# Reordering the head of a mixer stage and moving a gate table from GpSimd to VectorE

## The chip, the cores and the metric

The kernel runs on one core of a Trainium2 chip. A core has TensorE (PE: matmuls, and transposes through an identity matrix), VectorE (DVE), ScalarE (ACT), GpSimd (POOL) and SyncE (SP), each with its own instruction stream that is worked off in order. The engines meet through semaphores only. The metric is the device time of one execution in microseconds, lower is better.

## The reference

One layer of a decoder for 512 tokens of 1024 features, in f32:

```python
h = x + concat(GatedDeltaNet(u), RG_LRU(u)) @ W_out        # u = rmsnorm(x)
h = h + CrossAttn(rmsnorm(h), rmsnorm(mem))                # 4 heads, 256 memory tokens
h = h + MoE(rmsnorm(h))                                    # top 4 of 32 SwiGLU experts
out = rmsnorm(h)
```

The parts that the change touches are these:

```python
# gated delta rule, per head (4 heads of 128) and chunk
gcum = cumsum(g);  decay = exp(gcum_t - gcum_s) below the diagonal
A = strict_lower((k*beta) @ k.T * decay);  solve (I + A) [u, w] = [v*beta, k*beta*exp(gcum)]
qk = causal(q @ k.T * decay);  o = (q*exp(g)) @ S + qk @ v_new;  S = S*exp(g_last) + k_dec.T @ v_new
# RG-LRU, 4 blocks of 128 channels
r = sigmoid(x @ w_a + b_a);  i = sigmoid(x @ w_x + b_x)
a = exp(8 * r * log_sigmoid(lam));  h_t = a*h_{t-1} + sqrt(1 - a*a) * (i*x)
# routing and experts
logits = rmsnorm(h) @ w_router + b_router;  top_e, gate = top_k(4), softmax
out_e = ((clip(x@w_up+b_up)+1) * gt*sigmoid(1.702*gt)) @ w_down + b_down   # gt = min(x@w_gate+b_gate, 7)
y = sum over the 4 experts of gate * out_e
```

## The kernel before, in words

**Stages.** Front projections; then the mixer (gated delta rule and RG-LRU); the output projection; cross-attention; routing; a loop over blocks of 128 rows, each of one expert; and a last block that shares its end with the combination of the results and the final norm. Weights are f32 and are split on chip into a high and a low part in a reduced format (ACT rounds the high part, DVE subtracts for the low part), and each weight piece is multiplied as high x high, high x low and low x high.

**Order.** Nothing schedules the instructions. Each engine's program is written out by hand, with a `wait_ge(semaphore, count)` ahead of what needs another engine's result and a `then_inc` behind what releases one. So where an instruction stands in its engine's text decides what it delays.

**The head of the mixer.** All heads work on 128-token chunks, four to a head (`[P, 4, P]` tiles of 128x512). PE first does the eight matmuls of the RG gates (L1175) into banks 6 and 7 of the accumulator memory, then for each head the matmul that sums log decays along a chunk (L1181, "decay sums"), for which DVE prepares the operand (L1709). DVE turns the sums into arguments (L1715 to L1719), ACT applies `exp` to them (L828, L829, L833). Then come four products per head on PE (`kk`, `kq`, and two transposes: L1199, L1201, L1203, L1205), and DVE multiplies each with its decay or scale (L1729 to L1739). POOL cuts the triangles with `affine_select` (L502, L504), and builds the masked matrix of a level (L523). The two `fill_wait` calls (L1120) issue dummy matmuls that nothing reads.

**The inverse.** `(I + A)` is inverted in seven levels. Level one is `I - mask*A` for each head (DVE L1744, transposed on PE L1215, copied by ACT L845). The six others are a loop of 24 steps, one per level and head, with two matmul groups and a transpose on PE (L1227, L1239, L1247), two copies on ACT (L852, L855) and a subtraction on DVE. In the first twelve steps DVE also does the RG-LRU (three steps per block). ACT's `tanh` and `exp` of the RG gates (L818, L821) stand ahead of the decay exponentials; its `sqrt` (L859) stands in the loop. A change of function set shows as ACT_TABLE_LOAD.

**Routing.** In the last projection of the cross-attention (PE L1304, weights split by ACT L713 and DVE L1616), four tiles of the result are added to the residual (DVE L1812), transposed (PE L1404), copied to SBUF by `evac_h2` (DVE L1883) and multiplied with the router weights (PE L1411). These steps are put between the pieces by the piece number `c`.

**The expert loop.** SP loads three 4 MB weight matrices per block into a ring (L426). POOL issues the indirect transfers and, block by block, the load of the biases (L629) for PE's bias matmul (L1496). Ahead of the loop's first bias load POOL works out `g_parts` (L608 to L614): per token a row of 32 with the four gate values at their experts. Only the last block needs it, for `y`'s bias term. In the last block DVE splits weight pieces (L1888), adds a bias (L2045), clamps and multiplies (L2056, L2058) and makes the low part of the hidden values (L2061). PE transposes with L1533 and multiplies with L1546.

## Time and profile before

| | us |
|---|---|
| median of 3 runs | 1771.23 (1770.09 to 1771.25) |
| the profiled execution | 1772.93, of which the span is 1771.2 |
| PE busy / DVE busy / ACT busy / POOL busy | 1690.2 / 1437.0 / 1274.6 / 527.8 |
| chain that ended last: PE / DVE / issue / ACT / POOL | 61% / 18% / 12% / 6% / 3% |

The profile is of one execution. A row of a timeline has the start, the busy time of a run of equal instructions, and in brackets the idle time of that engine ahead of it with the instruction that ended it. `PEclk` is the clock that TensorE was granted, as a share of full speed; half speed shows as 0.50. The share of each engine over the whole span says little, since most of the span is the expert loop and the change is in four short places.

### The profile page before, as it was taken

To read this page: it belongs to the slowest core of one execution; us is meant where nothing else is said; L and a number is where in the kernel's file an instruction comes from. 1 tells how busy PE (TensorE), PEld (TensorE's weight loads), DVE (VectorE), ACT (ScalarE), POOL (GpSimd) and SP (SyncE) were. 2 spreads that over 40 slices of the span, in tenths; PEclk is the share of its full clock that TensorE was granted. 3 is DMA by queue.
4 is the path that set the end of the run, shared out by engine and by line. 5 is a ranking of instruction groups with operands and counts; after the bars stand their busy time and mean duration, and the time that the engine had idled before them with its cause. 6 is when DMAs were issued, how large, how long until landed. Compare 5 with 4: busy or idle time off the path is not lost.

```text
span 1771.2 us, 24520 instructions
## 1 busy us (share of the span) xinstructions
PE 1690.2 (95%) x8065; PEld 1385.7 (78%) x8065; DVE 1437.0 (81%) x1531; ACT 1274.6 (72%) x1452; POOL 527.8 (30%) x624
## 2 busy tenths in 40 slices
PE   6999799899899989999999999999999999999997
PEld 3778598787768768888888888888888888888885
DVE  3558686663347969999999999999999999999997
ACT  4453454464435668888888888888888888888885
POOL 3453552200022822242222222232232323232232
PEclk9999999999998989999999999999999999999999
DMA  7312100042014879999999999999999999999993
GB/s 249 119 51 100 41 1 1 24 190 95 26 82 191 330 271 369 360 383 378 355 371 371 382 359 370 360 382 379 351 371 369 379 364 369 360 380 379 353 371 120
DMA packets 53880, 476.18 MB, mean 269 GB/s; under 512 B 10503, under 2 KB 11640, under 8 KB 29266
## 3 DMA queue, kind: packets, MB, share of 16 engines
q1 hardware_dynamic: 42528, 450.70, 62.8%
q0 software_dynamic: 11120, 24.91, 6.3%
q8 instruction: 25, 0.41, 0.1%
q14 instruction: 13, 0.11, 0.0%
q10 hardware_dynamic: 194, 0.06, 0.0%
HBM read 461.24 MB, written 23.08 MB: 273 GB/s over the span
## 4 chain that ended last, share of the span: by engine, by line
PE 61%; DVE 18%; issue 12%; ACT 6%; POOL 3%; DMA 1%; ACTq 0%; POOLq 0%; DVEq 0%
PE ps L1546 20%; PE ps L1506 17%; PE ps L1143 10%; PE ps L1304 4%; DVE wsp L1888 4%; DVE extra L2058 2%; DVE extra L2056 2%; DVE wsp_b L1888 2%; ACT extra L1048 2%; POOL extra L608 1%; PE ps L1533 1%; PE ps L1227 1%; DVE wf L1616 1%; PE ps L1239 1%; PE ps L1496 1%
## 5 line engine op out<-in xcount | busy, mean ns | idle before, releaser
L1888 DVE TENSOR_TENSOR wsp<-ring,wsp 128x1024 fp32r<-128x1024 f32 x512 | 601.1, 1219 | 26.6 <-ACT wsp L1003 26.1
L1003 ACT ACTIVATE wsp<-ring 128x1024 fp32r<-128x1024 f32 x388 | 387.0, 1051 | 80.2 <-PE ps L1488 53.0
L580 POOL TENSOR_TENSOR guard<-guard 1x1 f32<-1x1 f32 x219 | 133.8, 616 | 763.0 <-ACT extra L1071 327.9
L1506 PE MATMUL ps<-wsp,x_hi 128*128 128x512 f32 x1152 | 311.8, 392 | 0.6 <-DVE x_lo L2014 0.6
L1888 DVE TENSOR_TENSOR wsp_b<-ring,wsp_b 128x1024 fp32r<-128x1024 f32 x256 | 301.8, 1218 | 9.8 <-ACT wsp_b L1081 9.1
L1506 PEld LDWEIGHTS ps<-wsp,x_hi 128*128 128x128 f32 x1152 | 217.5, 189 | 50.1 <-issue 1.1
L1003 ACT ACTIVATE wsp_b<-ring 128x1024 fp32r<-128x1024 f32 x194 | 205.5, 1060 | 32.3 <-PE ps L1506 11.0
L1506 PE MATMUL ps<-wsp,x_lo 128*128 128x512 f32 x576 | 179.1, 392 | 0.0
L1616 DVE TENSOR_TENSOR wf<-ring,wf 128x1024 fp32r<-128x1024 f32 x64 | 81.3, 1273 | 111.8 <-ACT wf L713 111.8
L713 ACT ACTIVATE wf<-ring 128x1024 fp32r<-128x1024 f32 x80 | 84.2, 1055 | 117.4 <-PE ps L1143 62.2
L1143 PE MATMUL ps<-act_hi,wf 128*128 128x512 f32 x512 | 161.6, 397 | 2.6 <-DVE wf L1616 2.1
L1081 ACT ACTIVATE wsp<-ring 128x1024 fp32r<-128x1024 f32 x124 | 131.9, 1064 | 36.8 <-PE ps L1546 36.8
L1546 PE MATMUL ps<-wsp_b,hid_hi 128*128 128x512 f32 x512 | 140.2, 395 | 0.0
L1506 PE MATMUL ps<-wsp_b,x_hi 128*128 128x512 f32 x512 | 136.8, 389 | 0.0
L1546 PE MATMUL ps<-wsp,hid_hi 128*128 128x512 f32 x512 | 136.8, 389 | 0.0
L1506 PEld LDWEIGHTS ps<-wsp,x_lo 128*128 128x128 f32 x576 | 108.6, 189 | 23.4
L1488 PE MATMUL ps<-wsp,x_hi 128*128 128x512 f32 x384 | 118.2, 389 | 0.0
L1143 PEld LDWEIGHTS ps<-act_hi,wf 128*128 128x128 f32 x512 | 95.7, 188 | 27.5 <-issue 8.1
L1546 PEld LDWEIGHTS ps<-wsp,hid_hi 128*128 128x128 f32 x512 | 96.1, 188 | 20.0
L1506 PEld LDWEIGHTS ps<-wsp_b,x_hi 128*128 128x128 f32 x512 | 96.1, 188 | 20.0
L1546 PEld LDWEIGHTS ps<-wsp_b,hid_hi 128*128 128x128 f32 x512 | 93.6, 188 | 22.8 <-issue 4.8
L1143 PE MATMUL ps<-act_lo,wf 128*128 128x512 f32 x256 | 99.8, 390 | 0.0
(380 smaller groups left out, 2993.9 us busy)
## 6 DMA issues: line engine op xcount, KB each, us to landing
ring<-in_w_gate_dram SPq DMA_DIRECT2D x32, 4096.0 KB, 15.3
ring<-in_w_up_dram SPq DMA_DIRECT2D x32, 4096.0 KB, 14.4
ring<-in_w_down_dram SPq DMA_DIRECT2D x32, 4096.0 KB
ring<-in_w_in_dram SPq DMA_DIRECT2D x6, 2048.0 KB, 12.0
ring<-in_w_ckv_dram SPq DMA_DIRECT2D x4, 2048.0 KB, 10.1
ring<-in_w_out_dram SPq DMA_DIRECT2D x2, 2048.0 KB, 10.6
ring<-in_w_cq_dram SPq DMA_DIRECT2D x2, 2048.0 KB, 11.1
ring<-in_w_co_dram SPq DMA_DIRECT2D x2, 2048.0 KB, 10.6
```

The lines of the kernel that those rows point to most:

```text
L580: return pool.tensor_tensor(guard[:, i:i + 1], guard[:, 0:1], guard[:, 0:1], ALU.mult)
L713: act.activation(parts_of(f, 0), piece(f), ACT.Copy).then_inc(wfh_ready, 1)
L1003: act.activation(split_w(c, 0), ring[:, m, k], ACT.Copy).then_inc(hi_ready, 1)
L1048: act.activation(gs, ps[:, 0:2, :].rearrange("p b f -> p (b f)"), ACT.Sigmoid, scale=1.702).then_inc(sg_ready, 1)
L1081: act.activation(split_w(c, 0), ring[:, GM, c], ACT.Copy).then_inc(hi_ready, 1)
L1143: last = pe.matmul(o, parts_of(f, w)[:, k], a[:, k], start=(k == 0 and w == 0 and a is a_hi), stop=(k == KT - 1 and a is a_lo))
L1304: last = pe.matmul(ps[:, banks[b]], a[:, rows + kk, ts], parts_of(f, w)[:, kk], start=(first and kk == 0 and a is a_hi and w == 0), stop=( ...
L1488: o = pe.matmul(ps[:, bank + i], xp[:, c % KT * P:(c % KT + 1) * P], split_w(c, w)[:, i * 512:(i + 1) * 512], start=False, stop=(last_k an ...
L1506: last = pe.matmul(ps[:, 2 * j + i], xp[:, k * P:(k + 1) * P], split_w(c, part)[:, i * 512:(i + 1) * 512], start=False, stop=(k == KT - 1 ...
L1546: last = pe.matmul(ps[:, 4 + i], xp[:, k * P:(k + 1) * P], split_w(c, part)[:, i * 512:(i + 1) * 512], start=(k == 0 and xp is hid_hi and ...
L1616: dve.tensor_tensor(parts_of(f, 1), piece(f), parts_of(f, 0), ALU.subtract).then_inc(wfl_ready, 1)
L1888: dve.tensor_tensor(split_w(c, 1), ring[:, (GM + c // KT) % 3, c % KT], split_w(c, 0), ALU.subtract).then_inc(lo_ready, 1)
```

## The change

1. PE: the decay sums stand ahead of the RG gate matmuls. Those go into banks 0 and 1, two or four at a time, between the products of the heads. The transposes of the first level follow head by head in the same stretch (into banks 2, 3, 6 and 7). Both `fill_wait` calls (30 and 34 dummy matmuls) are gone. The level loop's first steps wait for one head each and not for all four.
2. ACT: the decay exponentials stand ahead of the gates' sigmoids. `tanh` and `exp` of the gates move into the level loop (`tanh` in steps 0 to 3, `exp` in steps 3 and 5).
3. POOL: the `affine_select` of `a_m` is dropped, that of `qkt` moves into the masks of level 2. The mask of the first level is done head by head. Two of four gated inputs move behind masks of the loop.
4. DVE: `first_level(h-1)` follows the products of head h; DVE waits for the decays and not for the triangles.
5. DVE: the second `evac_h2` stands at c == 10 and not at c == 11.
6. The gate table is removed from POOL and built by DVE with 15 instructions ahead of the last block's `expert_lo`.

In the diff a part of the indentation is left off.

```diff
@@
...
         y_m, qkt = extra[:, 0:4], extra[:, 4:8]
+        D_A, D_K, D_Q = (1, 4, 7, 9), (2, 5, 8, 10), (3, 6, 11, 12)
+        X1_BANK = (2, 3, 6, 7)
         def onrm(h):
@@
         pool.tensor_tensor(b_lo, b_f, b_hi, ALU.subtract).then_inc(bias_split, 1)
-for n in range(4):
+def gated_input(n):
     pool.wait_ge(ri_ready, 2 * n + 2)
     pool.tensor_tensor(chan[:, 16 + n], chan[:, 16 + n], act_t[:, 4 + n], ALU.mult).then_inc(bx_ready, 1)
+def level_mask(l, h):
+    pool.tensor_tensor(quart(as_m[:, (4 * l + h) % 2]), quart(a_m[:, h]),
+                       lmask[:, l:l + 1, :].to_broadcast([P, 4, P]), ALU.mult).then_inc(as_ready, 1)
 for h in range(H):
-    pool.wait_ge(decay_ready, 3 * h + 2)
...
+    pool.wait_ge(decay_ready, D_Q[h])
     pool.wait_ge(kk_done, 4 * h + 2)
...
-pool.wait_ge(kk_evac, 4 * H)
-for l in range(7):
+    pool.wait_ge(kk_evac, 4 * h + 1)
+    pool.wait_ge(gb_done, H)
+    if h >= 2:
+        pool.wait_ge(x1_ready, h - 1)
+    level_mask(0, h)
+gated_input(0)
+gated_input(1)
+for l in range(1, 7):
     for h in range(H):
         i = 4 * l + h
...
-                           lmask[:, l:l + 1, :].to_broadcast([P, 4, P]), ALU.mult).then_inc(as_ready, 1)
+        if i - 4 >= 2:
+            pool.wait_ge(qm_done, i - 5)
+        else:
+            pool.wait_ge(x1_ready, H)
+        level_mask(l, h)
+        if i in (5, 6):
+            gated_input(i - 3)
+        if l == 2:
+            pool.wait_ge(kk_evac, 4 * h + 2)
+            pool.affine_select(out=quart(qkt[:, h]), in_=quart(qkt[:, h]), compare_op=ALU.is_ge, fill=0.0,
+                               base=0, pattern=[[0, 4], [1, P]], channel_multiplier=-1).then_inc(masked_ready, 1)
 for h in range(H):
@@
 link(take(0, tok_tab, slice(CAP, CAP + 1)))
...
-pool.wait_ge(codes_ready, 2)
...
-for t in range(0, NT, 2):
-    for u in range(2):
-        for k in range(TOPK):
-            last = pool.tensor_scalar(one[:, u, k], e_row, top_e[:, t + u, k:k + 1], gates[:, t + u, k:k + 1], ALU.is_equal, ALU.mult)
-    link(last)
...
@@
         sums_of(j - 6)
-act.wait_ge(proj_done, 24)
+act.wait_ge(gp_ready, 1)
+act.activation(egp, gp, ACT.Exp).then_inc(kdf_ready, 1)
+def q_decay(h):
+    act.wait_ge(kd_in, h + 1)
+    if h >= 2:
+        act.wait_ge(qexp_ready, h - 1)
+    act.activation(q_m[:, h % 2], ps[:, h], ACT.Exp).then_inc(decay_ready, 1)
+for h in range(H):
+    act.wait_ge(split_ready, h + 1)
+    act.activation(a_m[:, h], a_m[:, h], ACT.Exp, scale=-1.0).then_inc(decay_ready, 1)
+    act.activation(qkt[:, h], qkt[:, h], ACT.Exp).then_inc(decay_ready, 1)
+    if h < 2:
+        q_decay(h)
+act.wait_ge(kd_in, H)
+act.activation(kdf, kdf, ACT.Exp).then_inc(kdf_ready, 1)
+q_decay(2)
+q_decay(3)
 for n in range(4):
     for g in range(2):
         act.wait_ge(gate_mm, 2 * n + g + 1)
         r = (R_BA if g == 0 else R_BX) + n
-        act.activation(act_t[:, 4 * g + n], ps[:, 6 + g], ACT.Sigmoid, bias=par[:, r:r + 1]).then_inc(ri_ready, 1)
...
-for n in range(4):
+        act.activation(act_t[:, 4 * g + n], ps[:, g], ACT.Sigmoid, bias=par[:, r:r + 1]).then_inc(ri_ready, 1)
+def rg_tanh(n):
     act.wait_ge(bx_ready, n + 1)
     act.activation(act_t[:, 4 + n], act_t[:, n], ACT.Tanh, scale=nrate[:, n:n + 1]).then_inc(rt_ready, 1)
-act.wait_ge(rt_ready, 4)
-for n in range(4):
+def rg_exp(n):
+    act.wait_ge(rt_ready, n + 1)
     act.activation(act_t[:, n], act_t[:, n], ACT.Exp, scale=rate[:, n:n + 1]).then_inc(rt_ready, 1)
...
 def rg_hi(n):
     act.wait_ge(rg_done, n + 1)
@@
     if 2 <= i < 22:
         act.wait_ge(x1t_done, H + i - 1)
         act.activation(x_m[:, (i - 2) % 4], ps[:, 3 * (i % 2) + 2], ACT.Copy).then_inc(x_lev, 1)
+    if i < 4:
+        rg_tanh(i)
+    if i in (3, 5):
+        rg_exp(i - 3)
+        rg_exp(i - 2)
     if i in (4, 7, 10, 13):
         n = i // 3 - 1
         act.wait_ge(mult_in, n + 1)
@@
         pe.matmul(ps[:, 6 + i % 2], ones[:], chan[:, 16 + i], start=True, stop=True).then_inc(l2_done, 1)
-pe.wait_ge(rgw_in, 32)
-pe.wait_ge(tile_done, 20)
-for n in range(4):
-    for g in range(2):
-        if n > 0:
-            pe.wait_ge(ri_ready, 2 * (n - 1) + g + 1)
-        pe.matmul(ps[:, 6 + g], rgw[:, g, n], chan[:, 16 + n], start=True, stop=True).then_inc(gate_mm, 1)
 pe.wait_ge(tile_done, 24)
 for h in range(H):
     pe.wait_ge(gu_ready, h + 1)
     pe.matmul(ps[:, h], ones[:], as_m[:, h % 2], start=True, stop=True).then_inc(gb_done, 1)
-pe.wait_ge(qk_ready, 2 * H)
-for h in range(H):
-    if h == 1:
-        pe.wait_ge(decay_ready, 3)
-        pe.wait_ge(kd_in, 1)
-        fill_wait(30, 0)
+def rg_gates(n):
+    for g in range(2):
+        if n > 0:
+            pe.wait_ge(ri_ready, 2 * (n - 1) + g + 1)
+        pe.matmul(ps[:, g], rgw[:, g, n], chan[:, 16 + n], start=True, stop=True).then_inc(gate_mm, 1)
+def head_products(h):
...
         last.then_inc(kk_done, 1)
-pe.wait_ge(decay_ready, 3 * H)
-pe.wait_ge(kd_in, H)
-fill_wait(34, 0)
-for h in range(H):
+def first_inverse(h):
     pe.wait_ge(x1_ready, h + 1)
...
     last.then_inc(x1t_done, 1)
+pe.wait_ge(qk_ready, 2 * H)
+head_products(0)
+pe.wait_ge(rgw_in, 32)
+pe.wait_ge(decay_ready, D_Q[1])
+rg_gates(0)
+head_products(1)
+head_products(2)
+pe.wait_ge(decay_ready, D_Q[3])
+pe.wait_ge(kd_in, H)
+first_inverse(0)
+rg_gates(1)
+head_products(3)
+first_inverse(1)
+rg_gates(2)
+rg_gates(3)
+pe.wait_ge(kk_evac, 4 * H)
+first_inverse(2)
+first_inverse(3)
+pe.wait_ge(ri_ready, 8)
 def level_q(i):
...
     if i < 4:
-        pe.wait_ge(y1_ready, 4)
+        pe.wait_ge(y1_ready, i + 1)
     else:
         pe.wait_ge(y_lev, i - 3)
...
@@
...
 dve.wait_ge(beta_ready, 1)
-dve.wait_ge(kdf_ready, 2)
+dve.wait_ge(kdf_ready, 1)
 link(dve.tensor_tensor(beg, beta, egp, ALU.mult))
+def first_level(h):
+    dve.wait_ge(as_ready, h + 1)
+    dve.tensor_tensor(quart(x_m[:, h]), ident[:].unsqueeze(1).to_broadcast([P, 4, P]), quart(as_m[:, h % 2]), ALU.subtract).then_inc(x1_ready, 1)
 for h in range(H):
...
     dve.wait_ge(kk_done, 4 * h + 1)
-    dve.wait_ge(masked_ready, 2 * h + 1)
+    dve.wait_ge(decay_ready, D_A[h])
...
     dve.wait_ge(kk_done, 4 * h + 2)
-    dve.wait_ge(masked_ready, 2 * h + 2)
+    dve.wait_ge(decay_ready, D_K[h])
...
     dve.wait_ge(kk_done, 4 * h + 3)
...
+    if h == 0:
+        dve.wait_ge(kdf_ready, 2)
...
     dve.wait_ge(kk_done, 4 * h + 4)
     dve.tensor_tensor(quart(chan[:, 8 + h]), quarters(7), bc(beta), ALU.mult).then_inc(kk_evac, 1)
-for h in range(H):
-    dve.wait_ge(as_ready, h + 1)
...
+    if h >= 1:
+        first_level(h - 1)
+first_level(3)
 for i in range(24):
     h = i % 4
     dve.wait_ge(p_done, i + 1)
-    dve.wait_ge(y1_ready, 4)
+    dve.wait_ge(y1_ready, min(i + 1, 4))
...
         if i % 3 < 2:
@@
     if c == 9:
         evac_h2(0, 0, 4, 1)
         evac_h2(0, 1, 5, 2)
-    if c == 11:
+    if c == 10:
         evac_h2(1, 0, 6, 3)
         evac_h2(1, 1, 7, 4)
     if c == 13:
@@
...
+def gate_table():
+    one = extra[:, 5, 256:512].rearrange("p (t k e) -> p t k e", t=2, k=TOPK)
+    for t in range(0, NT, 2):
+        for u in range(2):
+            ins = dve.tensor_tensor(one[:, u], e_row.unsqueeze(1).to_broadcast([P, TOPK, E]),
+                                    tf4[:, t + u].unsqueeze(2).to_broadcast([P, TOPK, E]), ALU.is_equal)
+        link(ins)
+        for u in range(2):
+            ins = dve.tensor_tensor(one[:, u], one[:, u], gates[:, t + u].unsqueeze(2).to_broadcast([P, TOPK, E]), ALU.mult)
+        link(ins)
+        for u in range(2):
+            ins = dve.tensor_reduce(g_parts[:, t + u, 2 * E:3 * E], one[:, u].rearrange("p k e -> p e k"), AX_X, ALU.add)
+        link(ins)
+    for c in range(2):
+        ins = dve.tensor_copy(g_parts[:, :, E * c:E * (c + 1)].bitcast(F32R), g_parts[:, :, 2 * E:3 * E])
+    link(ins)
+    dve.tensor_tensor(g_parts[:, :, 2 * E:3 * E], g_parts[:, :, 2 * E:3 * E], g_parts[:, :, 0:E], ALU.subtract).then_inc(iota_ready, 1)
 def expert_lo(n, last=False):
...
@@
     for c in range(NSPLIT):
...
+gate_table()
 expert_lo(n_more, last=True)
 dve.wait_ge(bias_split, 4)
...
```

PE's order at the head of the mixer, before: 1175 are the gates, 1181 the decay sums, 1120 the dummies, 1199 to 1205 a head's products.

```order
L1175 MATMUL ps<-chan,xn 128x512 x8
L1181 MATMUL ps<-ring,ones 128x512 x4
L1199 MATMUL ps<-chan 128x128 x4
L1201 MATMUL ps<-chan 128x128 x4
L1203 MATMUL ps<-ident,chan 128x128 x4
L1205 MATMUL ps<-ident,chan 128x128 x4
L1120 MATMUL ps<-sel 128x256 x30
L1199 MATMUL ps<-chan 128x128 x4
```

The same place now: 1179 are the decay sums, 1198 to 1204 a head's products, 1187 the gates, 1211 the first level's transposes.

```order
L1179 MATMUL ps<-ring,ones 128x512 x4
L1198 MATMUL ps<-chan 128x128 x4
L1200 MATMUL ps<-chan 128x128 x4
L1202 MATMUL ps<-ident,chan 128x128 x4
L1204 MATMUL ps<-ident,chan 128x128 x4
L1187 MATMUL ps<-chan,xn 128x512 x2
L1198 MATMUL ps<-chan 128x128 x4
L1200 MATMUL ps<-chan 128x128 x4
```

The eight gate matmuls no longer stand ahead of the decay sums, and the dummies are gone. ACT's order at the start of the level loop, before: 845 copies the first level, 852 and 855 are the loop's copies, 859 the square root.

```order
L845 ACTIVATE extra<-ps 128x512 x4
L852 ACTIVATE ring<-ps 128x512 x3
L855 ACTIVATE ring<-ps 128x512
L852 ACTIVATE ring<-ps 128x512
L855 ACTIVATE ring<-ps 128x512
L852 ACTIVATE ring<-ps 128x512
L855 ACTIVATE ring<-ps 128x512
L859 ACT_TABLE_LOAD
L859 ACTIVATE act_t<-act_t 128x512
```

The same place now: 854 and 857 are the copies, 834 a `tanh`, 838 an `exp`, 866 a square root.

```order
L854 ACTIVATE ring<-ps 128x512
L857 ACTIVATE ring<-ps 128x512
L834 ACTIVATE act_t<-act_t,small 128x512
L838 ACT_TABLE_LOAD
L838 ACTIVATE act_t<-act_t,small 128x512 x2
L854 ACTIVATE ring<-ps 128x512
L857 ACTIVATE ring<-ps 128x512
L866 ACT_TABLE_LOAD
L866 ACTIVATE act_t<-act_t 128x512
L854 ACTIVATE ring<-ps 128x512
L857 ACTIVATE ring<-ps 128x512
L838 ACT_TABLE_LOAD
```

Eight activations and three table loads now stand between the loop's copies. DVE's order around the second `evac_h2`, before: 1616 is the low part of a weight piece, 1812 the addition to the residual, 1883 the copy of `evac_h2`.

```order
L1598 RECIPROCAL small<-small 128x1
L1616 TENSOR_TENSOR wf<-ring,wf 128x1024
L1812 TENSOR_TENSOR resid<-resid,ps 128x512 x2
L1883 COPY chan<-ps 128x4x128 x2
L1616 TENSOR_TENSOR wf<-ring,wf 128x1024 x2
```

The same place now, where 1633 is the low part, 1838 the addition and 1909 the copy.

```order
L1615 RECIPROCAL small<-small 128x1
L1909 COPY chan<-ps 128x4x128 x2
L1633 TENSOR_TENSOR wf<-ring,wf 128x1024
L1838 TENSOR_TENSOR resid<-resid,ps 128x512 x2
L1633 TENSOR_TENSOR wf<-ring,wf 128x1024 x2
```

The two copies stand ahead of one weight piece and one addition that they stood behind.

## Rows read from the trace of the kernel before

**Rows 1.** Windows: start:end, length, busy PE, PEld, DVE, ACT, POOL, PEclk, DMA share, GB/s

```profile
218.00:220.00 2.00, 1.39 (x7) 0.99 (x5) 0.00 (x0) 1.17 (x2) 1.95 (x2) 0.50 0.00 0
...
222.00:276.00 54.00, 53.09 (x457) 51.94 (x456) 46.42 (x53) 30.41 (x52) 29.68 (x22) 0.98 0.00 1
...
627.60:666.80 39.20, 39.01 (x165) 31.94 (x166) 31.66 (x30) 31.38 (x33) 8.51 (x14) 0.92 0.72 259
666.80:703.00 36.20, 36.05 (x166) 29.65 (x165) 33.59 (x33) 31.18 (x33) 8.74 (x14) 1.00 0.94 368
```

**Rows 2.** Timeline of PE, the bias matmul of block 1

```profile
627.64 1.22 PE L1496 MATMUL ps<-bias,sel 128*128 128x512 f32 x2 [10.47 <-DMA bias<-bias_parts]
```

**Rows 3.** Timeline of POOL ahead of the expert loop

```profile
585.42 17.80 POOL L608 TENSOR_SCALAR extra<-extra,gates 128x32 f32<-128x32 f32 x8
...
616.97 1.31 POOL L614 TENSOR_TENSOR extra<-extra 128x128 f32<-128x128 f32 x1
...
623.37 0.59 POOL L629 DMA_DIRECT2D bias<-bias_parts  x1 [0.44 <-issue]
```

**Rows 4.** DMA issues: what, queue, kind, count, KB each, us to landing

```profile
gate_rows<-gates SPq DMA_DIRECT2D x1, 8.0 KB, 9.9
```

**Rows 5.** Timeline of SP, first expert weights and gates

```profile
584.69 0.37 SPq L419 DMA_DIRECT2D gate_rows<-gates  x1
...
614.27 0.37 SPq L426 DMA_DIRECT2D ring<-in_w_down_dram  x1
```

**Rows 6.** Chain of waits around the router: start, length, what

```profile
532.11 0.87 PE ps L1404 x8
...
543.39 5.20 PE ps L1304 x12
548.59 1.71 PE ps L1411 x16
...
551.20 2.77 PE ps L1304 x12
```

**Rows 7.** Timeline of PE at the router

```profile
540.62 2.77 PE L1411 MATMUL ps<-w_rt,chan 128*128 128x32 f32 x16 [2.18 <-DVE chan L1883]
```

**Rows 8.** Timeline of DVE at the router

```profile
533.52 1.21 DVE L1616 TENSOR_TENSOR wf<-ring,wf 128x1024 fp32r<-128x1024 f32 x1
...
536.85 1.23 DVE L1616 TENSOR_TENSOR wf<-ring,wf 128x1024 fp32r<-128x1024 f32 x1 [2.04 <-ACT wf L713]
...
539.19 1.28 DVE L1883 COPY chan<-ps 128x512 f32<-128x512 f32 x2
```

**Rows 9.** Timeline of DVE at the head of the mixer

```profile
186.56 2.26 DVE L1709 TENSOR_TENSOR ring<-tri,small 128x512 f32<-128x512 f32 x2 [5.46 <-PE ps L1181]
...
196.13 0.77 DVE L1723 TENSOR_TENSOR small<-small 128x16 f32<-128x16 f32 x1 [1.03 <-ACT small L836]
...
210.05 0.68 DVE L1739 TENSOR_TENSOR chan<-ps,small 128x512 f32<-128x512 f32 x1
```

**Rows 10.** Timeline of PE, start of the level loop

```profile
220.17 2.04 PE L1227 MATMUL ps<-extra,ring 128*128 128x128 f32 x8 [0.78 <-ACT extra L845]
```

**Rows 11.** Timeline of ACT, functions of the RG gates

```profile
186.35 2.56 ACT L818 ACTIVATE act_t<-act_t,small 128x512 f32<-128x512 f32 x4
188.92 1.28 ACT L821 ACT_TABLE_LOAD   x1
```

**Rows 12.** Timeline of DVE, one-hot rows of the routing, and the last block

```profile
563.00 0.49 DVE L1920 TENSOR_TENSOR extra<-extra 128x128 f32<-128x128 f32 x2
563.52 0.69 DVE L1924 TENSOR_REDUCE extra<-extra 128x32 f32<-128x128 f32 x2
...
1721.23 4.78 DVE L1888 TENSOR_TENSOR wsp<-ring,wsp 128x1024 fp32r<-128x1024 f32 x4
...
1730.20 1.23 DVE L2045 TENSOR_TENSOR extra<-ps,extra 128x1024 f32<-128x1024 f32 x1
```

**Rows 13.** Timeline of PE near the last block's end

```profile
1742.23 0.75 PE L1533 MATMUL ps<-ident,extra 128*128 128x128 f32 x4 [0.80 <-DVE extra L2058]
```

More of the change, by code:

```diff
@@ L354, in build_layer @@
         nf_row, bd_rows, bd_parts = ring[:, GM, 0, :], ring[:, GM, 1, :], split_w(0, 0)
+        e_row = extra[:, 4, 384:384 + E]
         g_parts, g_stack = extra[:, 4, 0:NT * 3 * E].rearrange("p (t c) -> p t c", t=NT), bias4[0:3 * E, T:2 * T]
@@ L546, in _ @@
             link(pool.tensor_copy(ef[:, 288:418], it_i[:, 288:418]))
-            e_row = extra[:, 4, 384:384 + E]
             link(pool.tensor_copy(ef[:, 0:E], it_i[:, 0:E]))
@@ L601, in _ @@
             gather()
-            pool.wait_ge(codes_ready, 2)
-            top_e = extra[:, 5, 128:160].rearrange("p (t k) -> p t k", t=NT)
-            one = extra[:, 5, 256:512].rearrange("p (t k e) -> p t k e", t=2, k=TOPK)
-            for t in range(0, NT, 2):
-                for u in range(2):
-                    for k in range(TOPK):
-                        last = pool.tensor_scalar(one[:, u, k], e_row, top_e[:, t + u, k:k + 1], gates[:, t + u, k:k + 1], ALU.is_equal, ALU.mult)
-                link(last)
-                link(pool.tensor_tensor(one[:, :, 0:2], one[:, :, 0:2], one[:, :, 2:4], ALU.add))
-                link(pool.tensor_tensor(g_parts[:, t:t + 2, 2 * E:3 * E], one[:, :, 0], one[:, :, 1], ALU.add))
-            for c in range(2):
-                link(pool.tensor_copy(g_parts[:, :, E * c:E * (c + 1)].bitcast(F32R), g_parts[:, :, 2 * E:3 * E]))
-            pool.tensor_tensor(g_parts[:, :, 2 * E:3 * E], g_parts[:, :, 2 * E:3 * E], g_parts[:, :, 0:E], ALU.subtract).then_inc(iota_ready, 1)
             link(pool.memset(gate_sb[:], 0.0))
@@ L844, in _ @@
                 act.wait_ge(x1t_done, h + 1)
-                act.activation(y_m[:, h], ps[:, h], ACT.Copy).then_inc(y1_ready, 1)
+                act.activation(y_m[:, h], ps[:, X1_BANK[h]], ACT.Copy).then_inc(y1_ready, 1)
             for i in range(24):
@@ L1206, in _ @@
                     last.then_inc(kk_done, 1)
-            pe.wait_ge(decay_ready, 3 * H)
-            pe.wait_ge(kd_in, H)
-            fill_wait(34, 0)
-            for h in range(H):
+            def first_inverse(h):
                 pe.wait_ge(x1_ready, h + 1)
                 for c in range(4):
-                    last = pe.transpose(quarters(h)[:, c], quart(x_m[:, h])[:, c], ident[:])
+                    last = pe.transpose(quarters(X1_BANK[h])[:, c], quart(x_m[:, h])[:, c], ident[:])
                 last.then_inc(x1t_done, 1)
+            pe.wait_ge(qk_ready, 2 * H)
[17 more added lines that the diff above has]
+            pe.wait_ge(ri_ready, 8)
             def level_q(i):
@@ L1266, in _ @@
             pe.wait_ge(wt_ready, 4)
+            pe.wait_ge(masked_ready, H)
             for c in range(NT):
@@ L1739, in _ @@
                 dve.tensor_tensor(quart(chan[:, 8 + h]), quarters(7), bc(beta), ALU.mult).then_inc(kk_evac, 1)
-            for h in range(H):
-                dve.wait_ge(as_ready, h + 1)
-                dve.tensor_tensor(quart(x_m[:, h]), ident[:].unsqueeze(1).to_broadcast([P, 4, P]), quart(as_m[:, h % 2]), ALU.subtract).then_inc(x1_ready, 1)
+                if h >= 1:
+                    first_level(h - 1)
+            first_level(3)
             for i in range(24):
@@ L1754, in _ @@
                     if i % 3 == 0:
-                        dve.wait_ge(rt_ready, 8)
+                        dve.wait_ge(rt_ready, n + 1)
                         dve.wait_ge(gate_mm, 8)
@@ L1770, in _ @@
                     elif i % 3 == 1:
+                        dve.wait_ge(rt_ready, 5 + n)
                         link(dve.tensor_tensor_scan(act_t[:, 4 + n], act_t[:, n], chan[:, 16 + n], 0.0, ALU.mult, ALU.add))
```

28 lines of the change are left out of this document (removed).

## The prediction

> **What bounds the kernel now.** I read the windows first. In the level loop of the mixer PE works 53.09 of 54.00 us, and in a block of the expert loop 36.05 of 36.20 [rows 1]: both are bound by PE, and the change removes no product from either. So time can only go where PE waits, and the PE timelines and the chain of waits were read for that, at the four places of the edit.
>
> Start of the expert loop: PE idles 10.47 us at 627.64 for the bias of block 1 [rows 2]. POOL issues that DMA at 623.37, because it builds the gate table first, from 585.42 to 618.28 [rows 3]. The window of block 1 is 39.20 long at a granted clock of 0.92, the next 36.20 at 1.00 [rows 1]: after the stall PE ran at half clock (1.2 of 2.4 GHz) for a while.
>
> Router: PE idles 2.18 us at 540.62 for DVE's second `evac_h2` [rows 7], whose copies start at 539.19 behind a weight piece and an addition, although the transposes that they copy ended at 532.98 [rows 6, 8].
>
> Head of the mixer: DVE wrote its first two operands by 181.10 and idled 5.46 us for PE's first decay sum, which stood behind the gates; at 196.13 it waited 1.03 more for ACT [rows 9], which first did four `tanh`, a table load and four `exp` [rows 11]. The level loop began at 220.17 [rows 10].
>
> Last block: DVE is fuller than elsewhere. From 1721.23 to 1730.20, 8.97 us, it does seven pieces of about 1.14 (4.63 to 4.78 for four), 7.95 us [rows 12], so some 1.0 us is free; soon after, PE waits 0.80 for DVE's L2058 [rows 13].
>
> **A. Table off POOL: -13.4.** POOL comes to the loop's first bias load without the 32.86 us from 585.42 to 618.28. It first waits for the gate rows to be written: issued at 584.69, landing 9.9 later [rows 4, 5], at 594.6. Its steps from the table's end to the bias issue took 623.37 - 618.28 = 5.1, so the issue comes at 599.7; the landing took at most 627.64 - 623.37 = 4.3, so 604.0. PE could have used the bias at 627.64 - 10.47 = 617.17. The cover is 13 us. The whole stall goes (10.47), and with it the half-clock stretch: 39.20 - 36.20 = 3.00, of which I count 2.9, since blocks differ by 0.1. What would be late next is a weight matrix. The third of block 1 is issued at 614.27 [rows 5]; 4 MB at the loop's 368 GB/s [rows 1] are 11.4 us, so it is there by about 628 with its latency, and is used in the last third of the block, from 641. Bounds: -10.5 (the clock falls all the same) to -13.5.
>
> **B. Second `evac_h2` one piece earlier: -5.7.** DVE is free at 533.52 + 1.14 = 534.7 and idles until 536.85, and the pair of copies takes 1.28 [rows 8]: done by 536.0, ahead of the 538.44 (540.62 - 2.18) at which PE wants them. The 2.18 go. The stall was followed by half clock: the router matmuls took 2.77 and those of the next group 5.20, against 1.71 and 2.77 later [rows 6]. That gives back 1.06 and 2.43. Sum 5.67. Nothing behind the copies comes later: they fill an idle time, and the piece at 536.85 keeps its place. Bounds: 0 (PE then waits for the next low part instead) to -5.7; the nearest row is the stall itself, so I take the latter.
>
> **C. Mixer: -7.5.** Start: without the gates ahead, the first decay sum runs when DVE has written its operand, about 181.1, so DVE's second pair of L1709 starts some 4.7 to 5.2 earlier (a sum itself lasts under 1 us). The 1.03 for ACT goes, because the decay exponentials come first. Of L1723's 0.77 for sixteen elements a part may go too, which I put at 0 to 0.6. So the products of the heads begin 7.0 earlier (6.3 to 7.3): at 189.9, not 196.9. Before, they ended at 210.73 [rows 9], 13.8 for four heads. Now four first-level subtractions of 0.6 stand between them (2.4), and PE's gate matmuls and POOL's masks fall into the same stretch: 2.0 for stalls, by estimate, between 0 and 1.0 for each head. End 208.1. From the last product to the loop lay 220.17 - 210.73 = 9.4, mostly masks, subtractions and transposes one behind another; of that only the last head's is left, 2.2, and 1.3 for POOL's gated inputs, which stand ahead of the first mask of the loop. The loop starts at about 211.5: -8.7, bounds -5 and -10.
>
> Loop: four `tanh`, four `exp` of 0.64 and three table loads of 1.28 [rows 11] are 9.0 us more for ACT in the first eight of 24 steps. ACT is busy 30.41 of 54.00 [rows 1], so in eight steps (18 us) about 8 are free, more in the first two, which have fewer copies. Only what comes at once delays PE: two `exp` behind a load, 2.6, against the 2.25 of a step (54.00 / 24). Twice 0.4 and a little for the third load is +1.2, with -2 and +3 as bounds: below nothing, since PE ran at half clock from before 218 until about 224 [rows 1], 2 us that need not recur.
>
> The Trainium skill speaks against this part: "ScalarE: Activation LUTs", section "Table sets: the hidden batching unit", asks for all `exp` together and then all square roots, and the change interleaves them. It puts a switch at about 2.7 us where the row has 1.28. By that price three loads are 8.1 and not 3.8, and the loop's share would be about +5 and not +1.2.
>
> **D. Table on DVE: +2.4.** Ahead of the last block stand 15 instructions in a chain. A pair of equality tests with 128x128 elements took 0.49 and a pair of reductions 0.69 [rows 12]; with a pair of products as the tests, and twice, that is 2 x (0.5 + 0.5 + 0.7) = 3.4, and the two copies and the subtraction, of the same size, add 0.6: 4.0 in all. Free in the last block are 1.0 before the bias addition and, by estimate, 0.6 after it; the rest, 2.4, reaches L2058, for which PE waits already [rows 13]. Bounds 0 (the splits run far enough ahead of PE) and +4.0.
>
> **Sum.** -13.4 - 5.7 - 7.5 + 2.4 = -24.2. The profiled execution took 1772.93, so 1748.7; it lay 1.7 above the median of the runs, so 1747.0. Its own range, with the terms' likely errors, is 1743 to 1751.
>
> **Rivals.**
> R1: the head of the mixer goes cold. The 64 dummies are gone, and PE has only a part of 190 to 208 to work in. For it: the clock is at 0.50 at 218 to 220 [rows 1], and at the router it fell after a wait of 2 us. Against: the fills did not prevent the former. A product of a head at half clock takes about 0.9 longer, four to eight groups on the path are +4, time 1751; if the first levels of the loop run so too, up to 1758.
> The Trainium skill, "TensorE: Matmul & The Clock Gate", part 1, says that idleness halves the clock and that only sustained work brings it back; the trace agrees, by the router matmuls of 2.77 behind the wait and 1.71 later.
> R2: DVE's delay in the last block makes PE idle about 2.4 at once, and the clock falls as at the router, whose fall cost 3.5: 1750.5.
> R3: the router gains nothing, because PE then waits for the delayed low part: 1747.0 + 5.7 = 1752.7. Against: DVE idles 2.04 just before that piece [rows 8].
> R4: the table is gone and block 1's bias is late all the same, since the gate rows' write queues behind weights. Then A is 0: 1760.4. Against: block 2's own bias, issued by the same code, made PE wait for nothing [36.05 of 36.20, rows 1].
> R5: ACT bounds the first steps of the loop. If only half of its 8 free us can be used, the 9.0 of additions cost +5 in place of +1.2: 1750.8. For it: each copy has a place in the order that it can't leave. Against: ACT has over 40% of the loop free. The Trainium skill, "ScalarE: Activation LUTs", in the section named above, would have it so.
> R6, the slower side: the level loop runs at half clock. PE fills it with small matmul groups; if ACT's additions open a gap in each of the first steps and the clock never comes back, the 54.00 us become up to 107, +53: 1800. It makes the kernel slower than before as soon as more than 24 us of level work at full clock run at half. Against: the loop of before recovered within some 7 us of its start.
>
> **How the numbers follow.** Forecast 0.49, R1 0.20, R2 0.08, R3 0.07, R4 0.05, R5 0.07, R6 0.04. Time 1747.0. 1741 takes the good ends of C and D together (-2.5 and -2.4 less about 1 for both at once); 1757 takes in R2, R3, R5 and nearly all of R1. A measurement of this kernel tells 0.2% (3.5 us) from no change. Faster needs less than 1767.7: all cases but R6, 0.96; same 0.01 and slower 0.03 are the two parts of R6.
>
> **What would show it.** A: no idle time at the bias matmul of block 1, the loop's first window at 36.2 and clock 1.00. B: idle at the first router matmuls under 0.2, and these at 1.7, the group behind them at 2.8. C: the L1709 pair without 5 us of idle, first level matmul near 211.5, and 54 to 57 us of levels. D: about 4.0 of table on DVE, and PE idle by about 3 in all in the last block. Wrong: PE at 0.50 between 190 and 230 for over 10 us; ACT's copies later than PE in more than the first eight steps; a new wait at the expert loop's start; or a last block longer by more than 4.

## The result, and the profile after

The changed kernel takes 1748.9 us (median of 4, 1747.36 to 1749.92) beside 1770.66 of the kernel before in the same comparison: a ratio of 0.9879, 95% interval [0.9867, 0.9891], 21.8 us. 1747.0 was predicted. The profiled execution took 1749.92 with a span of 1748.3, that is 22.9 less than the span before. The two profiled executions are each slower than the median of their kernel, the one of before by 2.3 us, so what a ledger of these two traces says is a little more than the medians say.

Windows of the changed kernel: the level loop, the second block of the expert loop, and a stretch of the last block (start:end, length, busy PE, PEld, DVE, ACT, POOL, granted clock, DMA share, GB/s).

```profile
211.12:268.50 57.38, 53.82 (x465) 52.25 (x465) 47.38 (x54) 38.88 (x63) 36.39 (x29) 1.00 0.01 1
603.45:639.70 36.25, 36.09 (x165) 29.68 (x164) 33.67 (x33) 31.22 (x33) 9.13 (x14) 1.00 0.95 372
1718.00:1722.00 4.00, 4.00 (x13) 3.14 (x13) 4.00 (x5) 2.14 (x3) 1.39 (x1) 0.57 0.00 0
```

The second expert block is 36.25 long and not 39.20, at clock 1.00 [rows 1]: the stall and what followed it are gone. The last row is new: half clock in the last block.

A ledger by stage. Each line has the start of one and the same PE instruction in both traces, and what the stage that ends there changed:

| up to | before | after | the part |
|---|---|---|---|
| first matmul of the chunk scan | 280.66 | 273.04 | mixer -7.62 |
| third group of router transposes | 550.12 | 536.90 | router -5.60 |
| first bias matmul of block 0 | 579.82 | 566.26 | -0.34 |
| first bias matmul of block 2 | 666.75 | 639.70 | start of the expert loop -13.49 |
| first bias matmul of the last block | 1717.52 | 1690.46 | -0.01 |
| end of the span | 1771.2 | 1748.3 | last block +4.16 |

Two lines hold more than the edit did, as the traces of the other kernels (e1 to e12, the experiments below) show. Of the mixer's -7.62, 0.74 lay ahead of it: the last projection matmul, which the change leaves alone, stood at 176.30 before and at 175.56 after. From it to the chunk scan are 104.36, 104.83 and 104.14 us in the three traces with the old order and its dummies (before, e1, e2), and 97.48, 97.47, 96.39 and 96.38 in the four with the new order as it is (after, e3, e4, e7): 6.7 to 8.4 us less. From the first bias matmul of block 0 to that of block 2 are 86.93 before, but 85.79, 84.74 and 85.08 in the other traces with the stall (e2, e3, e11), against 73.44 after: 11.3 to 13.5 us less.

PE at the head of the mixer and in the level loop:

```profile
179.89 6.47 PE L1179 MATMUL ps<-ring,ones 128*128 128x512 f32 x8 [3.95 <-DVE ring L1726]
...
211.12 2.33 PE L1243 MATMUL ps<-extra,ring 128*128 128x128 f32 x16 [0.74 <-issue]
...
224.31 1.16 PE L1255 MATMUL ps<-ring 128*128 128x128 f32 x8 [1.31 <-ACT ring L854]
...
227.22 1.16 PE L1255 MATMUL ps<-ring 128*128 128x128 f32 x8 [0.43 <-ACT ring L854]
...
230.83 1.16 PE L1255 MATMUL ps<-ring 128*128 128x128 f32 x8 [1.12 <-ACT ring L854]
```

The loop starts at 211.12 in place of 220.17 [rows 10]. Two prices stand beside it: PE idles 3.95 us where the gates were, the decay sums behind that run at half clock (6.47 for four of them), and in the loop PE waits three times for ACT. DVE in the same stretch:

```profile
182.04 0.69 DVE L1726 TENSOR_TENSOR ring<-tri,small 128x512 f32<-128x512 f32 x1 [1.70 <-PE ps L1179]
183.75 0.69 DVE L1726 TENSOR_TENSOR ring<-tri,small 128x512 f32<-128x512 f32 x1 [1.01 <-PE ps L1179]
...
191.50 1.13 DVE L1752 SCALAR_TENSOR_TENSOR ring<-ps,small,ring 128x128 f32<-128x128 f32 x4
...
205.81 0.68 DVE L1764 TENSOR_TENSOR chan<-ps,small 128x512 f32<-128x512 f32 x1
```

DVE's idle 5.46 [rows 9] has become 1.70 and 1.01, both for the sums. The router, and POOL ahead of the expert loop:

```profile
530.64 1.86 PE L1428 MATMUL ps<-w_rt,chan 128*128 128x32 f32 x16
...
535.20 1.86 PE L1428 MATMUL ps<-w_rt,chan 128*128 128x32 f32 x16
```

```profile
570.67 1.13 POOL L593 DMA_INDIRECT xg<-hn_rows,idx  x1 [0.91 <-POOL idx L601]
571.81 0.11 POOL L612 MEMSET gate_sb<- 128x1 f32 x1
581.53 0.45 POOL L601 TENSOR_TENSOR idx<-tabs 128x1 int32<-128x1 int32 x2 [9.61 <-issue]
...
584.80 0.59 POOL L626 DMA_DIRECT2D bias<-bias_parts  x1 [0.35 <-issue]
```

The router row has no bracket and its length is that of full clock; before it was 2.77 behind a wait of 2.18 [rows 7]. POOL waits 9.61 for the gate rows (their write was issued at 571.18 and takes 9.9, so it landed at about 581.1) and issues the bias load at 584.80, 18.7 us ahead of its use at 603.45. The last block, DVE and PE:

```profile
1694.18 0.49 DVE L2070 TENSOR_TENSOR extra<-extra 128x128 f32<-128x128 f32 x2
1694.71 0.50 DVE L2074 TENSOR_TENSOR extra<-extra,gates 128x128 f32<-128x128 f32 x2
1695.24 0.68 DVE L2077 TENSOR_REDUCE extra<-extra 128x32 f32<-128x128 f32 x2
...
1697.75 0.36 DVE L2080 CAST extra<-extra 128x128 fp32r<-128x128 f32 x2
1698.14 0.29 DVE L2082 TENSOR_TENSOR extra<-extra 128x128 f32<-128x128 f32 x1
```

```profile
1699.62 1.19 PE L1523 MATMUL ps<-wsp,x_hi 128*128 128x512 f32 x4 [0.32 <-DVE wsp L1914]
...
1715.71 0.75 PE L1550 MATMUL ps<-ident,extra 128*128 128x128 f32 x4 [1.17 <-DVE extra L2103]
1717.49 0.75 PE L1550 MATMUL ps<-ident,extra 128*128 128x128 f32 x4 [1.03 <-DVE extra L2103]
```

The table takes 1694.18 to 1698.35, 4.17 us. PE waits 1.17 and 1.03 where it had waited 0.80 once [rows 13], and the clock falls behind that: 0.57 from 1718 to 1722, where the same piece of the kernel before (1742.8 to 1746.8) had 1.00.

### The profile page after: what moved, and what is told of

Read it like the earlier page. It is cut to its first block, busy times and chain, and to the rows that moved or that the text cites. A ratio compares the mean times of both kernels' runs of the same rounds, so it can differ in the third digit from the quotient of the medians.

```text
span 1748.3 us, 24387 instructions
## 1 busy us (share of the span) xinstructions
PE 1677.2 (96%) x8001; PEld 1373.3 (79%) x8001; DVE 1438.7 (82%) x1546; ACT 1279.1 (73%) x1456; POOL 493.2 (28%) x597
## 4 chain that ended last, share of the span: by engine, by line
PE 61%; DVE 19%; issue 13%; ACT 6%; POOL 1%; DMA 0%; ACTq 0%; DVEq 0%; POOLq 0%
PE ps L1563 20%; PE ps L1523 17%; PE ps L1150 10%; DVE wsp L1914 5%; PE ps L1321 4%; DVE extra L2103 2%; DVE extra L2101 2%; DVE wsp_b L1914 2%; ACT extra L1055 2%; PE ps L1550 1%; DVE wf L1633 1%; PE ps L1255 1%; PE ps L1412 1%; PE ps L1513 1%; PE ps L1243 1%
```

## The experiments

A comparison with the kernel before has its own runs of it; medians are set beside 1770.06 (first four kernels), 1769.49 (next four) and 1770.85 (last four). Where a difference is near the spread of the runs, the verdict rests on traces.

**e1, e2, e3: each part alone.** The edits are the hunks of the diff: e1 only the table (POOL's lines out, `gate_table()` in), e2 only `c == 11` to `c == 10`, e3 only the mixer. What each of the mixer's own edits (PE, ACT, POOL, DVE) brings by itself was not run.

> The kernel before with only the gate table moved from POOL to DVE ahead of the last block. Theory (the parts add up, each at its own place): the stall of 10.47 us and the half-clock stretch at the expert loop's start go, -13.5, and the last block pays what it pays in the changed kernel, +4.2: -9.3, about 1761.4. Rival (the start of the loop is only free of the wait because the stages ahead came earlier too): the stall stays in part, and the gain is under 5 us. Rival on the price of the table (the prediction's +2.4): -11.0.

> The kernel before with only the second evac_h2 one piece earlier. Theory: the wait of 2.18 us at the first router matmul goes and the half-clock stretch behind it too: -5.6, about 1765.1. Rival: only the wait goes and the clock falls all the same, -2.2. Rival: DVE's later copies and additions come later, and nothing is gained.

> The kernel before with only the reordering of the mixer (PE, ACT, POOL, DVE). Theory: the chunk scan's first matmul comes 7.6 us earlier and nothing later changes: about 1763.1. Rival: the stages behind wait for weights that SP loads at their own pace, and less than 5 us arrive at the end.

Measured: 1761.08 (ratio 0.9945 [0.9929, 0.9962], -9.0), 1765.50 (0.9972 [0.9959, 0.9984], -4.6) and 1763.10 (0.9960 [0.9946, 0.9974], -7.0). The sum is -20.5 beside -21.8 for the whole in its own comparison: the parts add up within the spread. The rival of e1 falls (the stall is gone: 73.38 us from block 0 to block 2 in its trace). That of e3 is not excluded by the medians, whose interval reaches from 4.6 to 9.6 us; its trace has the mixer 6.9 shorter and the way from the chunk scan to the end not longer (1486.4 us, where before has 1490.5 and e11, with the same code there, 1486.9). The router part alone came out at 4.6, under the 5.6 of the ledger, but its interval reaches from 2.8 to 7.3, and e2's own trace has 263.82 from the chunk scan to the third group of router transposes where before had 269.46, 5.64 less. The router's wait is there in e1 and in e3, which keep the old place of `evac_h2`. PE in e1, then in e3:

```profile
539.93 1.94 PE L1398 MATMUL ps<-w_rt,chan 128*128 128x32 f32 x16 [2.18 <-DVE chan L1870]
...
544.53 1.86 PE L1398 MATMUL ps<-w_rt,chan 128*128 128x32 f32 x16
```

```profile
533.12 3.40 PE L1441 MATMUL ps<-w_rt,chan 128*128 128x32 f32 x16 [2.18 <-DVE chan L1922]
...
540.95 1.86 PE L1441 MATMUL ps<-w_rt,chan 128*128 128x32 f32 x16
```

The same wait of 2.18, but in e1 the clock did not fall: from one router group to the next 4.60 us, as in the changed kernel (4.56), against 7.83 in e3 and 7.80 before. So the wait costs 2.2 in some executions and 5.4 in others (2.18 and the 3.2 of the half clock). What taking it away gains in the mean depends on how often the clock falls, and four traces don't tell that.

**e4: the table ahead of the expert loop.**

```diff
+            gate_table()
             with dve.Fori(0, n_more) as n:
...
-            gate_table()
             expert_lo(n_more, last=True)
```

> The changed kernel with DVE's gate table ahead of the expert loop in place of ahead of the last block. Theory (the table costs what it exceeds DVE's free time at its place): the last block gets back 4.2 us, the first block has about 2.5 us free where the table now stands and pays 1.5, up to 3.3 if PE's clock falls: 1745.5 to 1748. Rival (the table's 4.0 us are on the path wherever DVE does them): the time stays at 1748.9.

Measured: 1748.01, ratio 0.9870 [0.9854, 0.9886]. The interval overlaps that of the changed kernel; the trace decides. From the last block's first bias matmul to the end 54.1 us, where the changed kernel has 57.8 and the kernel before 53.7. And in the first block, PE:

```profile
575.83 1.21 PE L1523 MATMUL ps<-wsp,x_hi 128*128 128x512 f32 x4 [1.53 <-DVE wsp L1914]
...
591.91 0.75 PE L1550 MATMUL ps<-ident,extra 128*128 128x128 f32 x4 [1.18 <-DVE extra L2103]
```

The wait of 1.53 is the one expected. With the second, which had been 0.16, the start of the loop became 3.06 longer (from the first bias matmul of block 0 to the second one of block 2, 87.91 against 84.85). The clock had no part in it: the granted clock was 1.00 in all of the block (windows from 564 to 604.7), although both waits are over 1 us; they lie 16 us apart. The table is paid where it stands, by what it exceeds DVE's free time; neither place is free.

**e7: the table cut in two.** The second half, the casts and the subtraction move behind the piece `lo(21)`, PE's transposes of the table behind the sixth piece of the down matrix, ACT's copy behind its last weight pieces.

```diff
-            gate_table()
+            gate_half(0)
             expert_lo(n_more, last=True)
...
                 lo(21, n * SPLIT + 22)
+                if last:
+                    gate_half(2)
+                    gate_rest()
...
+                    if last_block and k == 5:
+                        pe.wait_ge(iota_ready, 2)
+                        for t in range(NT):
+                            last = pe.transpose(ps[0:3 * E, 6, t * P:(t + 1) * P], g_parts[:, t], ident[:])
```

> The changed kernel with the gate table cut in two: half stands where it stood, and the other half with the casts and the subtraction behind the second piece of the down matrix, where DVE is three us ahead of PE; PE's transposes of it and ACT's copy follow later too. Theory (the table costs what exceeds DVE's free time at its place, and 1.6 of its 4.2 was the clock behind the wait): 0.5 to 1 is left of 4.2, so 1745.4. Rival (DVE is full anywhere in the last block): no gain, 1748.9, or slower because the transposes and the copy now stand just before the bias matmuls.

Measured: 1745.51, ratio 0.9863 [0.9846, 0.9879]. The last block's 57.84 became 54.36 (1691.74 to the span's 1746.1): 0.7 over before. PE there:

```profile
1716.23 0.74 PE L1545 MATMUL ps<-ident,extra 128*128 128x128 f32 x4 [0.79 <-DVE extra L2106]
...
1725.22 0.60 PE L1566 MATMUL ps<-ident,extra 128*96 128x128 f32 x4
```

One wait of 0.79, as before the change, and the late transposes wait for nothing. This shows both halves of the +4.16, the waits and the clock that they brought, but for a rest of 0.26 that is of another kind: from the bias matmuls behind the down matrix to the end it takes 17.65 to 17.75 us in all ten traces with the table on DVE, e4 and e7 among them, and 17.37 to 17.45 in the four with it on POOL. Its cause stays open.

**e5: dummies in PE's idle time ahead of the decay sums.**

```diff
+            pe.wait_ge(l2_evac, 8)
+            fill_wait(34, 6)
             pe.wait_ge(tile_done, 24)
```

> The changed kernel with 34 dummy matmuls (into bank 6) ahead of the decay sums, in PE's idle time of 3.95 us. Theory (the sums took 1.6 us each at half clock because PE had idled before them, and DVE waited 1.70 and 1.01 for them): they take 0.95, the products start 2 us earlier and the level loop 1.5 to 2 us earlier than 211.1: 1747.2. Rival (DVE and POOL bound the stretch, not the sums): no change, 1748.9.

Measured: 1747.15, ratio 0.9872 [0.9855, 0.9888]. PE:

```profile
176.81 4.24 PE L1127 MATMUL ps<-sel 128*128 128x256 f32 x34
180.92 3.94 PE L1181 MATMUL ps<-ring,ones 128*128 128x512 f32 x8
...
209.97 3.25 PE L1245 MATMUL ps<-extra,ring 128*128 128x128 f32 x16 [0.73 <-issue]
```

The sums take 3.94 in place of 6.47, and from their start to the level loop it is 29.05 us in place of 31.23: the theory's 2 us, there. In this execution the clock then was low at the loop's start (3.25 for what took 2.33), and from the sums to the chunk scan 91.77 are left, against 93.15 in the changed kernel's trace and 93.13, 92.04 and 92.06 in those of e3, e7 and e4, whose mixer is the same. So 0.3 to 1.4 us are left of it at the chunk scan. In e8 (below), which has the same dummies and the same mixer, the loop began at full clock (2.34) and 90.66 are left, 1.4 to 2.5 less. The medians alone don't tell the gain from none.

**e6, e9, e10: the order of exp and sqrt in the level loop.** The changed kernel has two exp in step 3 and two in step 5, between square roots. e6 has all four in step 3; e9 one in each of the steps 3, 5, 8, 11; e10 this:

```diff
-                if i in (3, 5):
-                    rg_exp(i - 3)
-                    rg_exp(i - 2)
-                if i in (4, 7, 10, 13):
-                    n = i // 3 - 1
+                if 4 <= i < 8:
+                    rg_exp(i - 4)
+                if i in (8, 9, 10, 13):
+                    n = (8, 9, 10, 13).index(i)
```

> The changed kernel with the four exp of the RG gates all in step 3 of the level loop, so that one pair of function-set switches less stands in the loop. Theory (what delays PE is what comes at once): one load of 1.28 and the return to the square root go, but four exp of 0.64 behind a load are 3.9 us in one piece against a step of 2.25, so PE's waits in the loop (2.9 us in three places) stay about as large: within 1 us of 1748.9. Rival (the number of switches decides, and each costs more than its own 1.28): 2.5 to 3 us faster, 1746.

> The changed kernel with one exp of the RG gates in each of the steps 3, 5, 8 and 11 of the level loop, so that exp and sqrt take turns four times: eight function-set loads in the loop and not four, and never more than 1.9 us in one piece. Theory (the size of a piece decides, the number of loads only adds ACT time that is free): PE's waits for ACT's copies in the loop (1.31, 0.43 and 1.12) shrink to 0.5 or less each but come up to eight times; from the decay sums to the chunk scan 91 to 93 us as in the changed kernel (92.0 to 93.2), and the time stays within 1 us of 1748.9. Rival (the number of loads decides): four more loads cost at least 5 us, 1754.

> The changed kernel with one exp in each of the steps 4 to 7 and the square roots in steps 8, 9, 10 and 13: two loads in the loop, no piece over 1.9 us. Theory (few loads and small pieces together): PE's waits for ACT's copies (2.9 us in all) nearly go, 2 to 2.5 us faster, 1746.6. Rival (something else, POOL's masks or DVE's reciprocals, sets these steps): the waits change their name and the time stays at 1748.9.

| | loads in the loop | largest piece (load and exp) | PE's waits for ACT in the loop | level loop | median, ratio |
|---|---|---|---|---|---|
| changed kernel | 4 | 2.6 | 1.31, 0.43, 1.12 | 57.38 | 1748.90, 0.9879 |
| e6 | 2 | 3.8 | 2.54 | 59.37 | 1751.02, 0.9893 [0.9876, 0.9909] |
| e9 | 8 | 2.0 | 0.70, 0.42, 0.52, 0.52, 0.52 | 57.94 | 1749.08, 0.9885 [0.9869, 0.9900] |
| e10 | 2 | 2.0 | none | 55.68 | 1748.64, 0.9882 [0.9867, 0.9897] |

The same loop differs from trace to trace by the clock at its start: the changed order has 57.06 to 57.38 in four traces that begin at full clock (after, e4, e7, e8), and 57.84 and 58.17 in two that don't (e3, e5). All three variants began at full clock. Neither the number of loads nor the size of a piece decides alone. With two loads, a piece of 3.8 (e6) gives a loop of 59.37 and pieces of 2.0 (e10) one of 55.68. With pieces of 2.0, eight loads (e9) give waits of 2.68 in all and 57.94, where two (e10) give none and 55.68. In the median e9 is where its theory had it, and its rival (5 us slower) fell; but that only the size counts is not borne out, since the sum of its waits is nearly that of the changed kernel (2.86). e10 has its square roots at other steps too, which no run separates from the rest. The timelines of e6 show how a large piece costs time, ACT's piece and then PE:

```profile
224.12 1.28 ACT L838 ACT_TABLE_LOAD   x1
225.41 2.56 ACT L838 ACTIVATE act_t<-act_t,small 128x512 f32<-128x512 f32 x4
227.88 0.58 ACT L854 ACTIVATE ring<-ps 128x512 f32<-128x512 f32 x1
```

```profile
228.51 1.85 PE L1255 MATMUL ps<-ring 128*128 128x128 f32 x8 [2.54 <-ACT ring L854]
```

The copy that PE needs stands behind 3.8 us of work, PE waits 2.54, and the group behind the wait takes 1.85 in place of 1.16, and the next two 1.06 and 1.63 in place of 0.60 and 1.06: the clock once more. The waits for ACT were as large as expected; the expectation for e6, within 1 us of 1748.9, left out the clock. The loop's 2.0 us are read from one trace; the medians (1751.02, and an interval that overlaps that of the changed kernel) point the same way without showing it. e10 has few loads and small pieces, and the waits for ACT are gone; only 0.89 for DVE is left in this part, and e12, which has the same order, repeats it (55.65, no wait for ACT):

```profile
227.62 0.66 PE L1262 MATMUL ps<-ident,extra 128*128 128x128 f32 x4 [0.89 <-DVE extra L1773]
```

Its loop is 1.7 shorter, but the median does not show it: whether 1.7 us arrive at the end in the mean stays open at this spread. Each load took 1.28 in all these rows.

**e11: the kernel before without its dummies.**

```diff
-                    fill_wait(30, 0)
...
-            fill_wait(34, 0)
```

> The kernel before without its 64 dummy matmuls (30 ahead of the second head's products, 34 ahead of the first level's transposes), nothing else. Theory (the first thirty stood on the path's edge and the others did not keep the clock up in front of the level loop, where it fell all the same): within 1 us of before. Rival (they keep the clock at full through the products): the clock falls from 194 on, and the kernel is 4 us slower or more.

Measured: 1770.65, ratio 1.0004 [0.9995, 1.0013]: no change that the runs show. The clock fell: 0.64 from 194 to 200 and 0.85 from 200 to 208. PE:

```profile
197.36 2.04 PE L1198 MATMUL ps<-chan 128*128 128x128 f32 x8 [5.27 <-DVE ring L1727]
...
213.99 1.94 PE L1213 MATMUL ps<-ident,ring 128*128 128x128 f32 x8 [5.97 <-DVE ring L1742]
...
220.15 3.75 PE L1225 MATMUL ps<-extra,ring 128*128 128x128 f32 x16 [0.78 <-ACT extra L845]
```

DVE bounds that stretch, but the products at half clock (2.04 for eight, 1.05 at full) made it wait twice. DVE:

```profile
201.15 0.69 DVE L1732 TENSOR_TENSOR extra<-ps,extra 128x512 f32<-128x512 f32 x1 [0.51 <-PE ps L1200]
202.00 0.69 DVE L1734 TENSOR_TENSOR chan<-ps,small 128x512 f32<-128x512 f32 x1 [0.16 <-PE ps L1202]
```

The loop starts at 220.15, as with the dummies (220.17), but this execution had been 0.8 us ahead at the end of the projections: from the last projection matmul to the loop it took 44.67 us, against 43.87 in each of before, e1 and e2. Its loop is longer as well, 57.04 against 55.95, 56.41 and 55.73, with the half clock lasting longer at its start. So in the trace the dummies were worth 0.8 us ahead of the loop and perhaps 1 in it. The medians don't show this; their interval, from 0.9 us faster to 2.3 slower, has room for it. The rival's price of 4 us is excluded.

**e8, e12: the better versions.** e8 is e5 and e7 together, e12 is e5, e7 and e10.

> The changed kernel with both of the two edits: the dummies ahead of the decay sums and the table cut in two. They lie 1500 us apart and should add up: 1743.7 if both theories hold; 1748.9 if neither does.

> The changed kernel with three edits: dummies ahead of the decay sums, the gate table cut in two, and one exp per step with the square roots behind them. If the parts add up: 1744 - 2.3 = 1741.8. Rival: with PE's waits in the loop gone DVE or POOL is the next bound, and it stays at 1744.

Measured: 1744.21 and 1743.75, both at 0.9856 [0.9840, 0.9873]. Both lie some 5 us under the changed kernel. e8 is where the two parts put it (1743.7); e12 is not at 1741.8 but near its rival's 1744. The third edit adds nothing that the runs tell from zero, though e12's trace has the shortest way from the sums to the chunk scan (180.40 to 269.65, 89.25).

## Why the prediction was right, point by point

**A, start of the expert loop**: predicted -13.4, measured -13.49 between the two profiled executions, and -11.3 to -13.5 with the other traces in place of that of before. The execution that the prediction was worked out from had the longest way through this place of the four, so the step was right for it and 1.0 to 2.1 us too large for the others. The bias load was issued 18.7 ahead of its use; with the 4.3 of its landing the cover is 14, where 13 had been worked out. The rival that the bias is late all the same, for the gate rows' write, fell: POOL waited 9.61 for that write, and PE did not wait for POOL.

**B, router**: predicted -5.7, ledger -5.60. The working assumed that the clock always falls behind the wait. e1 shows that it doesn't. The step was right for the profiled execution; whether it is too large for the mean the runs don't tell, since the 4.6 of e2's medians has an interval that holds 5.7 as well.

**C, mixer**: predicted -7.5, measured -7.62 in the ledger (-6.9 without the 0.74 from ahead of it), e3 -7.0. That it came so close is in part luck: errors cancelled inside. The products began 5.4 earlier (196.94 to 191.50) and not 7.0, because the gates had kept PE at full clock ahead of the sums, and without them PE idled 3.95 and ran the sums at half clock; I had given the sums under 1 us each, they took 1.6. The 7.0 had not followed from its own terms either: 4.7 to 5.2, 1.03, and 0 to 0.6 make 5.7 to 6.8. Against that the last product ended 15.0 us after the first began (191.50 to 206.49) and not 18.2. Of these 3.2, 2.0 are the stalls, which did not come, since PE and POOL kept ahead of DVE. The other 1.2 are two subtractions counted in the wrong place: `first_level(h-1)` follows the products of head h, so only two of the four stand ahead of the last product (L1745 at 198.35 and 202.38), and the other two behind it. That is why the tail behind the last product took 4.6 in place of 3.5. The loop began at 211.12 (211.5 predicted), and the loop was 1.43 longer (1.2 predicted, and some 5 with the dearer price of a load that the prediction gives beside it): waits of 2.86 for ACT, less the stretch of half clock at its start, which was gone.

**D, last block**: predicted +2.4, measured +4.16. This is the term that was mis-sized, and by the prediction's own list ("a last block longer by more than 4") a sign of being wrong. The table's duration was right (4.17 for 4.0), and so was what DVE's free time left of it: by the second transposes PE was 2.3 later, 0.6 of that already at the piece at 1699.62, which the prediction had not foreseen. Another 1.6 came between these and the bias matmuls behind the down matrix (1717.49 to 1730.61 against 1742.23 to 1753.77, 13.12 for 11.54), where the clock was 0.57 for 4 us, and 0.26 behind them (see e7). The 1.6 was rival R2, to which I gave 0.08 and 3.5 us. In the six traces with the whole table ahead of the last block it always came (57.6 to 57.9 us from the block's first bias matmul to the end), and in the three with half of it there, never (54.4). With R2 in the forecast at its measured 1.6 the number would have been 1748.6, at its own 3.5 it would have been 1750.5.

**The sum.** It gave -24.2 from a kernel of 1771.23, and the medians differ by 21.8. D is 1.8 of that, and A, sized on an execution above the median, about 1. The number came out nearer than the steps did. The lower end of the range has a slip: 2.5 and 2.4 less 1 below 1747.0 are 1743.1 and not 1741.

**The rivals.** R1, a cold head: right in its place (the sums) and small, since DVE's waits there are 2.7 us in all; e11 shows that the missing dummies cost little, and not nothing. R3, R4 and R6 fell. R5 is half right: ACT does hold up the first steps, by 2.9, and both the size of a piece and the number of loads count there. On the rule of the Trainium skill ("ScalarE: Activation LUTs", section "Table sets: the hidden batching unit", all of one set together): e6 follows it and is the slowest, e10 follows it one function at a time and has the shortest loop. In this loop the rule was worth following only with the pieces kept under a step (2.25 us).

## What to carry to other kernels

Work that leaves an engine's path is worth the stall plus the half-clock stretch behind it, and work put on another engine costs what exceeds that engine's free time at its place, plus the stretch behind the new wait: size both ends with the clock in them, and cut the work so that no wait of about 1 us comes twice in a row. Moving filler work (here the gates) away from an idle TensorE makes what follows slow, even if it starts earlier. Where an in-order engine serves a loop, count the longest piece between two of its copies against the length of a step, and how many such pieces there are; the sum of what is added says less. And before a stage is credited with a difference of two traces, see how far the same stage differs between traces of kernels that share it: here up to 1 us in the mixer and 2 at the start of the expert loop.
